# Gate and up tiles of a feed-forward network from the fifth on as 2x2 blocks with seven block products for eight, with the split of the gated rows moved to the start of the down product

## The reference, cut to what matters

```python
D_FF = 256 * ((8 * D_MODEL // 3 + 255) // 256)      # 2816

def swiglu(x, w_gate, w_up, w_down):
    return (jax.nn.silu(x @ w_gate) * (x @ w_up)) @ w_down
...
    for l in range(DEPTH):
        h = rmsnorm(x, g[0])
        x = x + 0.5 * rmsnorm(swiglu(h, prm['ffn_w_gate'][l, 0], prm['ffn_w_up'][l, 0],
                                     prm['ffn_w_down'][l, 0]), g[1])
```

## Time and profile before

| | |
|---|---|
| median of 3 runs | 2695.02 us (2690.11 to 2697.88) |
| profiled execution, its span from first to last instruction | 2698.6 us |
| TensorE busy in that span | 2640.3 us, 98% |
| VectorE, GpSimd, ScalarE busy | 1000.9, 888.3, 762.2 us |

### The profile page before, as it was taken

The page is one execution under the profiler, slowest core; times in us unless marked ns, Lnnn a source line. Parts: engine busy times, 40 slices in busy tenths (PEclk is TensorE's granted clock), DMA queues, the critical chain, the costliest instruction groups (busy, mean ns, idle before and its releaser), DMA issues.

```text
span 2698.6 us, 48666 instructions
## 1 busy us (share of the span) xinstructions
PE 2640.3 (98%) x21094; PEld 2580.8 (96%) x21094; DVE 1000.9 (37%) x1489; ACT 762.2 (28%) x1108; POOL 888.3 (33%) x440
## 2 busy tenths in 40 slices
PE   8999999999899999999999999999998999999998
PEld 8999999999789999999999999998987899999998
DVE  6222201776774422210352221028666663222103
ACT  4222211322523322221332222123144233222211
POOL 5333333432113433333343333334312144333331
PEclk9999999999999999999999999999999999999999
DMA  4222222323102222222222222222230013222222
GB/s 121 70 78 70 75 72 73 84 57 100 39 3 72 75 73 74 73 73 73 75 71 70 78 70 73 79 73 72 63 101 16 22 53 86 78 70 78 72 72 68
DMA packets 356053, 188.40 MB, mean 70 GB/s; under 512 B 16330, under 2 KB 354086, under 8 KB 355912
## 3 DMA queue, kind: packets, MB, share of 16 engines
q1 hardware_dynamic: 355668, 186.25, 23.9%
q10 hardware_dynamic: 244, 0.08, 0.0%
HBM read 179.50 MB, written 6.80 MB: 69 GB/s over the span
## 4 chain that ended last, share of the span: by engine, by line
PE 91%; DVE 4%; DVEq 1%; ACT 1%; issue 1%; DMA 1%; ACTq 0%; SPq 0%; POOL 0%
PE ps L1552 27%; PE ps L1554 26%; PE ps L1553 26%; PE ps L1598 3%; PE ps L1541 1%; DVE xT L1032 1%; PE ps L2060 1%; DVE ps L1028 1%; PE ps L2078 1%; PE ps L1748 1%; DVE h_split L1052 1%; PE ps L2074 1%; PE ps L1571 0%; DVE sb_qkv L1420 0%; DVEq L1045 0%
## 5 line engine op out<-in xcount | busy, mean ns | idle before, releaser
L567 POOL TENSOR_TENSOR w_lo<-w_raw,w_hi 128x1024 fp32r<-128x1024 f32 (+1 forms) x330 | 780.1, 2366 | 1652.9 <-ACT w_hi L627 1651.6
L1552 PE MATMUL ps<-h_split,w_hi 128*128 128x384 f32 (+1 forms) x3520 | 1103.2, 313 | 0.7 <-POOL w_lo L567 0.7
L1554 PE MATMUL ps<-h_split,w_lo 128*128 128x384 f32 (+1 forms) x3520 | 1092.7, 310 | 0.0
L1553 PE MATMUL ps<-h_split,w_hi 128*128 128x384 f32 (+1 forms) x3520 | 1082.6, 308 | 0.0
L1554 PEld LDWEIGHTS ps<-h_split,w_lo 128*128 128x128 f32 x3520 | 667.4, 190 | 0.0
L1552 PEld LDWEIGHTS ps<-h_split,w_hi 128*128 128x128 f32 x3520 | 661.1, 188 | 6.4 <-issue 4.9
L1553 PEld LDWEIGHTS ps<-h_split,w_hi 128*128 128x128 f32 x3520 | 662.8, 188 | 0.4
L627 ACT ACTIVATE w_hi<-w_raw 128x1024 fp32r<-128x1024 f32 (+1 forms) x330 | 342.1, 1038 | 818.0 <-DMA w_raw<-in_ffn_w_down 375.4
L1114 DVE TENSOR_TENSOR scratch<-ps,square_sums 128x640 f32<-128x640 f32 x176 | 144.3, 824 | 753.1 <-PE ps L1554 750.5
L1552 PE MATMUL ps<-hidden_split,w_hi 128*128 128x384 f32 (+1 forms) x1344 | 419.7, 312 | 0.0
L1554 PE MATMUL ps<-hidden_split,w_lo 128*128 128x384 f32 (+1 forms) x1344 | 416.6, 310 | 0.0
(11 more groups left out here) (323 smaller groups left out, 2009.3 us busy)
## 6 DMA issues: line engine op xcount, KB each, us to landing
w_raw<-in_ffn_w_gate SPq DMA_DIRECT2D x88, 512.0 KB, 3.7
w_raw<-in_ffn_w_up SPq DMA_DIRECT2D x88, 512.0 KB, 3.8
w_raw<-in_ffn_w_down SPq DMA_DIRECT2D x64, 448.0 KB, 3.6
w_raw<-in_w_in SPq DMA_DIRECT2D x42, 512.0 KB, 4.0
w_raw<-in_ffn_w_down SPq DMA_DIRECT2D x32, 512.0 KB, 3.8
w_raw<-in_w_out SPq DMA_DIRECT2D x16, 512.0 KB, 3.9
token_rows<-in_x_prompt SPq DMA_DIRECT2D x4, 512.0 KB, 5.6
k_cache<-in_cache_sb_k SPq DMA_DIRECT2D x2, 1024.0 KB, 5.8
```

Of the source, the lines that this page charges most:

```text
L567: nc.gpsimd.tensor_tensor(WLO[s][:, 0:n], RAW[s][:, 0:n], WHI[s][:, 0:n].bitcast(F32), ALU.subtract).then_inc(sem(f"lo_ready{s}"), 1)
L1552: MM(out, hi, mov[:, 0, cols], start=first, stop=False)
L1553: MM(out, hi, mov[:, 1, cols], start=False, stop=False)
L1554: return MM(out, lo, mov[:, 0, cols], start=False, stop=last)
```

## The change

Pairs 0 to 3 stay as they are. From pair 4 on (WINO_FROM = 4, 18 pairs of each of the four networks) gate and up tile together are one product of a 2x2 block weight matrix with a 2x2 block token matrix: the input features are cut into a front and a rear half (KHALF = 4 chunks each), the tokens into an early and a late half (NHALF = 320 columns each), the output features into gate and up. Instead of eight block products there are seven (`summed_pair`, named P1 P6 P5 P7 P4 P2 P3 in the order in which they are issued), each of 4 chunks x 3 matmuls of 320 columns. The operands of P6 and P5, of P3 on the weight side and of P7 and P4 on the token side are sums and differences of blocks:

- The token sums are made once per network while pairs 1 to 3 run: `base_second` and `token_highs` on ScalarE, `token_sums` on VectorE. They use the PSUM banks of pair 1, and TensorE waits for `token_banks_read` ahead of pair 3.
- The weight sums are made for each pair, one pair ahead, in the PSUM banks that the next pair will use: `sums_high` on ScalarE, `weight_sums`, `extra_lows`, `fourth_weights` on VectorE, `sums_low` on GpSimd.
- The seven results are put together in `second_sum`, `third_sum`, `up_out`, `gate_sum` and `gate_out`.
- A gated row stays whole (`hidden`, written by `pair_gated`); its high and low part are made for all 22 rows when the last pair is on TensorE and after it (`row_high`, `row_low`), and the first tile of the down product waits for each row (`hidden_split` at r + 1).
- SP loads the up block ahead of the gate block in the loop, since it is free first.

```diff
+            def sums_low(n, i, c):
+                k, (ug, uu) = pair_count(n, i, c) + 1, pair_blocks(n, i, c)
+                gate, up = weight_slots(n, c)
+                pool.wait_ge(sem(f"hi_ready{gate}"), ug)
+                pool.wait_ge(sem("second_weights"), k)
+                low_half(gate, FRONT).then_inc(sem("front_low"), 1)
+                pool.wait_ge(sem(f"hi_ready{up}"), uu)
+                nc.gpsimd.tensor_tensor(WLO[up][:], RAW[up][:], WHI[up][:].bitcast(F32), ALU.subtract).then_inc(sem(f"lo_ready{up}"), 1)
+                pool.wait_ge(sem("fourth_high"), k)
+                nc.gpsimd.tensor_tensor(XLO[:, X4], XRAW[:, X4], XHI[:, X4].bitcast(F32), ALU.subtract).then_inc(sem("fourth_low"), 1)
+                low_half(gate, REAR).then_inc(sem(f"lo_ready{gate}"), 1)
...
+            def first_kept(n, i, c):
+                act.wait_ge(sem("p1_in"), pair_count(n, i, c) + 1)
+                A(P1S[:], bank(c, A_), ACT.Copy).then_inc(sem("p1_kept"), 1)
...
+            def sums_high(n, i, c, first=False):
+                k, (ug, uu) = pair_count(n, i, c) + 1, pair_blocks(n, i, c)
+                gate, up = weight_slots(n, c)
+                act.wait_ge(sem(f"raw_loaded{up}"), uu * 16)
+                act.wait_ge(sem("up_scaled"), i * 2 + (n * FT + c - 1))
+                A(weight_bank(c, B_), RAW[up][:, FRONT], ACT.Copy).then_inc(sem("a21_copied"), 1)
+                act.wait_ge(sem(f"raw_loaded{gate}"), ug * 16)
+                A(WHI[gate][:], RAW[gate][:], ACT.Copy).then_inc(sem(f"hi_ready{gate}"), 1)
+                act.wait_ge(sem("third_weights"), k)
+                A(WHI[up][:], RAW[up][:], ACT.Copy).then_inc(sem(f"hi_ready{up}"), 1)
+                act.wait_ge(sem("second_weights"), k)
                 if not first:
...
+                    act.wait_ge(sem("p5_in"), k - 1)
+                A(XHI[:, X1], weight_bank(c, B_), ACT.Copy).then_inc(sem("extra_highs"), 1)
+                if not first:
+                    act.wait_ge(sem("p6_in"), k - 1)
+                A(XHI[:, X2], weight_bank(c, D_), ACT.Copy).then_inc(sem("extra_highs"), 1)
+                act.wait_ge(sem("fourth_weights"), k)
+                A(XHI[:, X4], XRAW[:, X4], ACT.Copy).then_inc(sem("fourth_high"), 1)
...
+                act.wait_ge(sem("p6_in"), w)
+                for r in range(4):
+                    row_high(n, r)
+                round_down(l, f, 0)
...
+                pair_silu(n, i, 1)
+                act.wait_ge(sem("p3_in"), w)
+                for r in range(HI_TURNED, FT):
+                    if r == 17:
+                        round_down(l, f, 2)
+                    row_high(n, r)
...
+            def token_sums(n, l, f):
+                g = [vec(l, "norm_g", 4 * f * DC + c) for c in range(DC)]
+                dve.wait_ge(sem("token_base"), n + 1)
+                for c in range(KHALF):
+                    V.scalar_tensor_tensor(out=TURNED_RAW[:, FIRST, c, 1, :], in0=XT[:, c, EARLY], scalar=g[c], in1=TBANKS[:, c], op0=ALU.mult, op1=ALU.subtract)
...
+                V.tensor_tensor(TS_[:, THIRD, :, 1, :], TBANKS, TS_[:, THIRD, :, 0, :].bitcast(F32), ALU.subtract)
+                fence().then_inc(sem("token_banks_read"), 1)
...
+            def pair_gated(n, i, c):
+                dve.wait_ge(sem("silu"), i * 2 + (n * FT + c + 1))
+                V.tensor_tensor(by_half(HU[:, i * 2 + c, :]), two_banks(c, A_), by_half(HB), ALU.mult)
+                fence().then_inc(sem("hidden"), 1)
+            def weight_sums(n, i, c):
+                k, (ug, uu) = pair_count(n, i, c) + 1, pair_blocks(n, i, c)
+                gate, up = weight_slots(n, c)
+                dve.wait_ge(sem("a21_copied"), k)
+                dve.wait_ge(sem(f"raw_loaded{gate}"), ug * 16)
+                V.tensor_tensor(RAW[up][:, FRONT], RAW[gate][:, FRONT], weight_bank(c, B_), ALU.subtract)
+                fence()
+                V.scalar_tensor_tensor(out=weight_bank(c, B_), in0=weight_bank(c, B_), scalar=-1.0, in1=RAW[up][:, REAR], op0=ALU.mult, op1=ALU.subtract)
+                fence().then_inc(sem("third_weights"), 1)
+                V.scalar_tensor_tensor(out=weight_bank(c, D_), in0=weight_bank(c, B_), scalar=-1.0, in1=RAW[gate][:, FRONT], op0=ALU.mult, op1=ALU.subtract)
+                fence().then_inc(sem("second_weights"), 1)
...
+            def extra_lows(n, i, c):
+                k = pair_count(n, i, c) * 2
+                for x, b in ((X1, B_), (X2, D_)):
+                    dve.wait_ge(sem("extra_highs"), k + x + 1)
+                    V.tensor_tensor(XLO[:, x], weight_bank(c, b), XHI[:, x].bitcast(F32), ALU.subtract).then_inc(sem("extra_lows"), 1)
+            def fourth_weights(n, i, c):
+                V.tensor_tensor(XRAW[:, X4], RAW[weight_slots(n, c)[0]][:, REAR], weight_bank(c, D_), ALU.subtract)
+                fence().then_inc(sem("fourth_weights"), 1)
+            def row_low(n, r):
+                dve.wait_ge(sem("hidden_hi"), n * FT + r + 1)
+                V.tensor_tensor(HLO[:, r, :], HU[:, r, :], hidden_high(r).bitcast(F32), ALU.subtract)
                 fence().then_inc(sem("hidden_split"), 1)
 
...
+            def second_sum(n, i, c):
+                k = pair_count(n, i, c) + 1
+                dve.wait_ge(sem("p6_in"), k)
+                dve.wait_ge(sem("p1_kept"), k)
+                V.tensor_tensor(U2S[:], bank(c, B_), P1S[:], ALU.add).then_inc(sem("u2_kept"), 1)
+            def third_sum(n, i, c):
+                k = pair_count(n, i, c) + 1
+                dve.wait_ge(sem("p7_in"), k)
+                V.tensor_tensor(U3S[:], bank(c, B_), P1S[:], ALU.add)
+                fence()
+                V.tensor_tensor(bank(c, B_), bank(c, C_), U3S[:], ALU.add).then_inc(sem("c22_made"), 1)
+            def up_out(n, i, c):
+                dve.wait_ge(sem(f"block_used{weight_slots(n, c)[1]}"), pair_blocks(n, i, c)[1])
+                V.tensor_tensor(bank(c, D_), bank(c, D_), U3S[:], ALU.add)
+                fence()
+                V.tensor_tensor(by_half(HB), two_banks(c, D_), by_half(ACC[:]), ALU.mult)
+                fence().then_inc(sem("up_scaled"), 1)
+            def gate_sum(n, i, c):
+                dve.wait_ge(sem("p3_in"), pair_count(n, i, c) + 1)
+                V.tensor_tensor(bank(c, C_), bank(c, C_), U2S[:], ALU.add)
+            def gate_out(n, i, c):
+                fence()
+                dve.wait_ge(sem(f"block_used{weight_slots(n, c)[0]}"), pair_blocks(n, i, c)[0])
+                V.tensor_tensor(two_banks(c, A_), two_banks(c, A_), by_half(ACC[:]), ALU.mult)
+                fence().then_inc(sem("gate_scaled"), 1)
...
+            def pair_evac(n, i, c, first=False):
+                second_sum(n, i, c)
+                if first:
+                    fourth_low(n)
+                else:
+                    pair_gated(n, i, c - 1)
+                weight_sums(n, i, c + 1)
+                third_sum(n, i, c)
+                extra_lows(n, i, c + 1)
+                up_out(n, i, c)
+                gate_sum(n, i, c)
+                fourth_weights(n, i, c + 1)
+                gate_out(n, i, c)
...
+                second_sum(n, i, 1)
+                pair_gated(n, i, 0)
+                row_lows(n, (0, 1, 2))
+                third_sum(n, i, 1)
+                row_lows(n, (3,))
+                up_out(n, i, 1)
+                row_lows(n, (4, 5, 6))
+                gate_sum(n, i, 1)
+                gate_out(n, i, 1)
+                row_lows(n, (7, 8))
+                pair_gated(n, i, 1)
+                row_lows(n, range(9, FT))
...
+            def half_product(out, hi, lo, mov, first=True, last=True):
+                for c in range(KHALF):
+                    begin, finish = first and c == 0, last and c == KHALF - 1
+                    MM(out, hi[:, c, :], mov[:, c, 0, :], start=begin, stop=False, skip_group_check=True)
+                    MM(out, hi[:, c, :], mov[:, c, 1, :], start=False, stop=False, skip_group_check=True)
+                    end = MM(out, lo[:, c, :], mov[:, c, 0, :], start=False, stop=finish, skip_group_check=True)
+                return end
+            def summed_pair(n, i, c):
+                k, (ug, uu) = pair_count(n, i, c) + 1, pair_blocks(n, i, c)
+                gate, up = weight_slots(n, c)
+                pe.wait_ge(sem("hidden"), i * 2 + (n * FT + c - 1))
+                pe.wait_ge(sem("front_low"), k)
+                half_product(bank(c, A_), WHI[gate][:, FRONT], WLO[gate][:, FRONT], H[:, FRONT, :, EARLY]).then_inc(sem("p1_in"), 1)
+                pe.wait_ge(sem("extra_lows"), k * 2)
+                pe.wait_ge(sem("token_lows"), n + 1)
+                half_product(bank(c, B_), XHI[:, X2], XLO[:, X2], TS_[:, SECOND]).then_inc(sem("p6_in"), 1)
+                half_product(bank(c, C_), XHI[:, X1], XLO[:, X1], TS_[:, FIRST]).then_inc(sem("p5_in"), 1)
+                pe.wait_ge(sem(f"lo_ready{up}"), uu)
+                pe.wait_ge(sem("u2_kept"), k)
```

(26 more changed lines are left out.)

254 lines of the change are left out of this document (184 added, 70 removed).

## The result

The changed kernel takes **2600.14 us** in the median of four runs (2598.72 to 2600.99), the kernel before 2694.43 (2690.11 to 2697.88). The ratio is 0.965, with a 95% interval of 0.9635 to 0.9666. The forecast was 2601.

The account below looks back on a forecast made before the run. TensorE's matmuls were taken to bound the kernel. Per network -31.9 (loop) + 0.5 (pair 3) + 8.0 (splits) = -23.4, times four -94 us: profiled span 2605, median 2601 us; own range 2577 to 2630, 2566 to 2652 with rivals.

Parts of the forecast that it names:

- The loop: Pairs, 18 in each of four networks: 84 matmuls at 0.1478 us, 12.41 us instead of 14.19; -127.7 us.
- the fourth rival: Loop: 320-column matmuls have a shorter gap than the 256-to-384 line gives, VectorE's chain is the pair; 2545 us, chance 0.03.
- VectorE keeps up: Loop: VectorE's work stays hidden behind the matmuls, with 1.0 us to spare in 12.41 and a 1.5 us wait for P6.
- The first rival: Loop: VectorE and ScalarE set the pair at 13.0 us through costlier drains or waits; 2643 us, chance 0.17.
- GpSimd doesn't touch VectorE in the loop: Loop: VectorE instructions with an input in PSUM aren't held by GpSimd, only those with two SBUF inputs; no cost.
- the third rival: Loop: GpSimd and VectorE exclude each other there too, 16.1 us per pair; 2867 us, slower, chance 0.05.
- The splits: Start of the down product: four GpSimd blocks hold back row splits, 1.9 us each; row 21 late, 8.0 us per network.
- the 8 that the prediction named as a sign: Expected profile: TensorE waiting for row split L1346, 8 us per network, in tile 0 only, from row 9 on.
- The second rival: Row splits aren't late because the lock costs little; edges 4 x 1 instead of 34; 2571 us, chance 0.09.
- Pair 3: Ahead of pair 3 TensorE waits for its banks until the third token sum's low part is done; 0.5 us lost.
- The sum: Per network -31.9 + 0.5 + 8.0 = -23.4 us; times four -94 us, giving 2601 us.

Follow-up runs that it names:

- the kernel in turns: Changed kernel with the down blocks of output tiles 0 and 1 taken in turns on every engine and queue; 2567.47 us, ratio 0.9526.
- the kernel with the hold and the moved sum: Changed kernel, GpSimd holding two down blocks until all row splits are done, third token sum's low part ahead of four two-SBUF-operand sums; 2587.38 us.

## Why the prediction was right

- **The loop** (-127.7). It gave 72 x (14.19 - 12.33) = -133.9, 6 us more. The matmul cost 0.147, not 0.148, which is the 0.08 us per pair. The line through 256 and 384 columns was the right ruler, and the fourth rival falls. The formula for an isolated matmul in the Trainium skill's page "TensorE: Matmul & The Clock Gate", section Back-to-back issue gap, would have given an estimate of 0.136 and a pair of 11.41, which the trace does not show.
- **VectorE keeps up** (1.0 us to spare before P3, 1.5 before P6). It had 1.42 and 1.43. The run with one more instruction and the run with three more bracket the slack: 0.6 us is free and 2.3 us is not. The first rival was 1.4 us away, its chain the one that was named.
- **GpSimd doesn't touch VectorE in the loop.** The instructions take 0.49, 0.69 and 0.82 us beside GpSimd, as the prediction had them without it, and the three-operand form 0.70 where it put 0.75. The same instruction with two SBUF operands takes 2.69. Of the two readings in the Trainium skill's "GPSIMD Engine Reference", the one of its Specifications, contention with VectorE instructions of two SBUF inputs, is what this pair of runs shows; the third rival falls. Its price was a little high as well: fourteen instructions at the prediction's own durations are 9.2 us, not 9.8 (9.1 in the trace), which makes its pair 15.5 and its time some 2820. In the same passage GpSimd's three half blocks are 3.9 us, not 3.7; the total of 6.3 is right.
- **The splits** (8.0 us per network, 1.9 for each block). They cost 8.9 in the mean. The four blocks are 7.3 of it, 1.83 each by the run without them, where the prediction had 7.6. The 13 splits by themselves are 1.24, not 0.4: they begin 7.5 us behind the last P3, not 7.2, and one takes 0.95 us with its drain, not 0.90. The lower clock, for which the prediction had no term, is the last 0.4; it is also the larger part of why TensorE's waits for the splits are 4.5 us per network and not the 8 that the prediction named as a sign. The run without the blocks and the two kernels that hold blocks back show the cause, and the kernel in turns shows that the lateness matters only because of TensorE's order. The second rival (lock costs little) falls with the same numbers.
- **Pair 3** (0.5). TensorE waited 0.67 there.
- **The sum.** Stages: predicted -23.4 per network, measured -23.8 in the mean. The larger gain of the loop (1.5 per network) and the larger losses (0.9 and 0.2) nearly cancel, and 0.1 is left. That the two errors have opposite signs is luck.
- **One assumption wasn't named:** that the rest of the kernel keeps its time. Between the two profiled executions the mixers gave another 6.7 us. Part of the agreement with the median, 2600.14 against 2601, is therefore luck too: mixers of 446 to 456 us in executions of the same kernels are an uncertainty as large as the 0.3% of a measurement.

## What to carry to other kernels

In this kernel the product with fewer matmuls pays in full only while the sums that replace them keep an operand in PSUM; one instruction of 512 columns with two SBUF operands beside a busy GpSimd cost 1.08 us per pair, and 72 of them 78 of the 94 us. Of work that is put off to the next stage, ask at what rate that stage consumes it: here the best remedy was not a hold on GpSimd (9 to 15 us) but an order of the consumer that wants each row half as often, and it gave 33 us more for a changed list of blocks. Before reading a difference of a few us as a gain, split the span by stage and compare the parts that nobody changed, and inside a stage look at the granted clock.

## What the runs showed that was not expected

The length of an unchanged part varies with TensorE's granted clock. Where TensorE stops in the first mixer, the changed kernel's first profile has a pause of 1 us (518 to 519) and keeps the clock of 2.4 GHz:

```profile
518.00:519.00 1.00, 0.02 (x2) 0.04 (x1) 1.00 (x3) 0.88 (x3) 0.00 (x0) 1.00 0.00 0
```

The same kernel's second profile has a pause of 2 us at the same place, and then 1.2 GHz for some 3 us, with 6 matmuls in a us instead of 9:

```profile
518.00:519.00 1.00, 0.00 (x0) 0.00 (x0) 1.00 (x2) 0.99 (x2) 0.39 (x1) 1.00 0.05 15
519.00:520.00 1.00, 0.16 (x1) 0.19 (x2) 0.91 (x3) 0.90 (x2) 0.00 (x0) 1.00 0.82 199
...
523.00:524.00 1.00, 1.00 (x6) 1.00 (x5) 1.00 (x2) 0.90 (x3) 1.00 (x2) 0.50 0.00 0
```

Read in windows of 20 us, the first mixer has one below full clock in the first profile (0.91 in 840 to 860) and five in the second (0.91 four times, 0.83 once). Against full clock that is 1.8 us in the first and 10.6 in the second; the difference of 8.8 is close to the 8.4 us by which that mixer is longer. The Trainium skill ("TensorE: Matmul & The Clock Gate", Part 1) says that the chip's look at TensorE's activity runs freely and does not begin anew with a kernel; varying executions of one kernel agree with that, and so do the four networks of the kernel with the hold and the moved sum, where the same splits were followed by the low clock twice and by full clock twice. What sets the length of the pause is not settled: a VectorE instruction of 128 columns with two SBUF operands takes 2.47 us just ahead of it in the second profile, and a neighbouring one 2.49 in the first, so the exclusion by GpSimd seems to fall on another instruction, but no run here changed that alone.

Low clock also came in tile 0, where TensorE paused for splits. It cost 1.5 us in the profiled execution of the changed kernel and 3.2 in that of the kernel with the hold and the moved sum, and nothing in the first network of the changed kernel, where TensorE had to wait for the last row all the same.
